# Handing an activation tile over in quarters, two PSUM banks exchanged, and a final norm by token sums in a two-block float32 transformer kernel

## What the kernel computes

```python
# first block, per layer
h = rmsnorm(x, g_mix);  z = h @ w_in                 # 12 column groups
y_a = latent attention (lora norms, w_q_up, w_kv_up, rotary, causal softmax)
y_b = sc_b * causal_dwconv(sc_c * sc_h, w_sc)        # 3 taps
u   = causal_dwconv(cf_a * sigmoid(cf_g), w_cf, b_cf)  # 31 taps, 512 channels
y_c = silu(layernorm(u));  y_d = retention
x = x + concat(y_a, y_b, y_c, y_d) @ w_o
uf = causal_dwconv(rmsnorm(x, g_ffn) @ w_up, w_ffn_conv)
x = x + (silu(gate) * up) @ w_down
x = x + (p @ w_pe) * sigmoid(rmsnorm(x, g_pe) @ w_pg)
# second block, per layer: rmsnorm, w_in_2, four attention-like mixers, gates
x = x + mixed @ w_out_2
# at the end
out = rms_norm(x, final_norm_g_2)                    # mean over the channels of a token
```

## Time and profile before

| | us |
|---|---|
| median of 3 runs (range) | 3526.3 (3523.01 to 3529.35) |
| profiled execution | 3530.64 |
| its span, first to last instruction | 3528.8 |

### The profile page before, as it was taken

How to read it: one execution, slowest core, us unless ns; L and a number is a source line. 1 busy time by engine, 2 the same in 40 slices (tenths; PEclk the granted TensorE clock), 3 DMA queues, 4 the chain that set the end, 5 groups by cost and what they waited for, 6 DMA issues and landing times. The chain is left out here.

```text
span 3528.8 us, 55547 instructions
## 1 busy us (share of the span) xinstructions
PE 3441.4 (98%) x21156; PEld 3019.1 (86%) x21156; DVE 2642.3 (75%) x3441; ACT 1467.2 (42%) x1488; POOL 982.2 (28%) x763
## 2 busy tenths in 40 slices
PE   8999999999999999999999999999999999999998
PEld 7899888888888888998888888888888888888887
DVE  7876688787776768766887777867667766677775
ACT  5434444343433543344443434335444444444442
POOL 0751433121123426714322121214231004040004
PEclk9899999999999999999999999999999999999999
DMA  6344455555555544344555555555443445443453
GB/s 225 132 142 163 173 191 191 174 196 177 202 175 189 178 163 149 133 166 171 186 190 171 199 177 203 173 188 187 169 164 134 155 168 183 168 150 128 156 179 141
DMA packets 90063, 605.10 MB, mean 171 GB/s; under 512 B 10000, under 2 KB 10160, under 8 KB 28592
## 3 DMA queue, kind: packets, MB, share of 16 engines
q1 hardware_dynamic: 88992, 599.83, 48.7%
q10 hardware_dynamic: 912, 3.11, 0.2%
HBM read 600.80 MB, written 2.10 MB: 171 GB/s over the span
## 5 line engine op out<-in xcount | busy, mean ns | idle before, releaser
L549 PE MATMUL bank<-H,whi 128*128 128x512 f32 x6784 | 2419.6, 401 | 51.5 <-DVE H L1462 37.6
L553 PE MATMUL bank<-H,wlo 128*128 128x256 f32 x7552 | 2126.5, 282 | 0.0
L549 PEld LDWEIGHTS bank<-H,whi 128*128 128x128 f32 x6784 | 1282.8, 189 | 371.3 <-DVE wlo L1412 38.1
L1041 ACT ACTIVATE whi<-raw 128x2048 fp32r<-128x2048 f32 (+1 forms) x610 | 1095.5, 1796 | 1199.5 <-DMA raw<-in_slabs_down 268.2
L1412 DVE TENSOR_TENSOR wlo<-raw,whi 128x2048 fp32r<-128x2048 f32 (+1 forms) x610 | 1337.6, 2193 | 185.2 <-ACT whi L1041 181.4
L553 PEld LDWEIGHTS bank<-H,wlo 128*128 128x128 f32 x7552 | 1437.9, 190 | 0.5
L549 PE MATMUL bank<-G,whi 128*128 128x512 f32 x1408 | 495.4, 395 | 0.0
L466 POOL TENSOR_TENSOR sqtmp<-tmp 128x256 f32<-128x256 f32 x88 | 219.1, 2490 | 888.4 <-DVE tmp L1980 888.4
L553 PE MATMUL bank<-G,wlo 128*128 128x256 f32 x1408 | 396.1, 281 | 0.0
L549 PEld LDWEIGHTS bank<-G,whi 128*128 128x128 f32 x1408 | 264.7, 188 | 62.9
L553 PEld LDWEIGHTS bank<-G,wlo 128*128 128x128 f32 x1408 | 264.1, 188 | 0.0
(11 more groups left out here) (318 smaller groups left out, 2481.6 us busy)
## 6 DMA issues: line engine op xcount, KB each, us to landing
raw<-in_slabs_up SPq DMA_DIRECT2D x176, 1024.0 KB, 4.8
raw<-in_slabs_down SPq DMA_DIRECT2D x128, 704.0 KB, 4.0
raw<-in_slabs_wo SPq DMA_DIRECT2D x32, 1024.0 KB, 4.8
raw<-in_slabs_pg SPq DMA_DIRECT2D x32, 1024.0 KB, 4.8
raw<-in_slabs_gates SPq DMA_DIRECT2D x32, 1024.0 KB, 4.8
raw<-in_slabs_wout SPq DMA_DIRECT2D x32, 1024.0 KB, 4.8
raw<-in_slabs_sc SPq DMA_DIRECT2D x24, 1024.0 KB, 4.8
raw<-in_slabs_fox SPq DMA_DIRECT2D x24, 1024.0 KB, 4.8
```

The costliest lines, as they stand in the source:

```text
L549: pe.matmul(b[0:r.m, :], whi[:, n % RAW, w], r.src[:, k, :], start=at == 0, stop=False)
L553: last = pe.matmul(b[0:r.m, 0:T], wlo[:, n % RAW, w], r.src[:, k, 0:T], start=False, stop=at == r.kt - 1)
L1041: act.activation(whi[:, n % RAW, 0:w], raw[:, n % RAW, 0:w], ACT.Copy).then_inc(S("hi_ready"), 1)
```

## The change

Four edits. (1) The runs wo, last down, pg and wout get an unrolled tail of four slabs on every engine (`tail`). At the last slab of each, ACT writes high chunks 0 to 11 as PE frees H a quarter at a time (`h_free`, raised behind chunks 3, 7 and 11 of the last slab; no such wait after down, whose product doesn't read H), and chunks 12 to 15 behind the last slab; the rounding of the slab three ahead comes after both. DVE writes low chunks 0 to 11 before it waits for the last slab, evicts that slab, writes 12 to 15, and splits the slab ahead after that. (2) In pe, unit 0 goes to the slab banks, with a wait for the eviction of the slab that used each, unit 1 to the auxiliary ones. (3) The output norm: ACT scales the chunks by the gain during the last slab, squares chunk 15 itself; PE sums over partitions and chunks with tokens on partitions (two products with one column for POOL's 15 chunks, two for chunk 15), root and reciprocal are of 128x2 values, two products spread them, and DVE multiplies four times 128x1024. (4) Taps: 5 (was 4) in cfa, 3 (was 8) behind kv, qn, qr, 2 at each ret slab but the first (was 4 at the last two only).

```diff
     # Run.__init__
-        self.head = 0
+        self.head = self.tail = 0
+    HANDED = ("wo", "pg", "wout", "rg", "gates")
+        if key[0] in HANDED[:3] or key[0] == "down" and key[2] == NG - 1:
+            by[key].tail = 4
+        if key[0] in HANDED:
+            h_free[key] = 3 * len(h_free)
     # groups
-        full = (r.count - tail) // 4 if r.loop else 0
+        full = (r.count - max(tail, r.tail)) // 4 if r.loop else 0
     # SP, output; POOL, last sum
-            sp.wait_ge(S("final_chunk"), 4 * k + 4)
+            sp.wait_ge(S("final_four"), k + 1)
-            square_sum(slab_of(("wout", l)))
+            square_sum(slab_of(("wout", l)), DC if l == 0 else DC - 1)
     # PE, run
-                    if key[0] in ("gates", "rg") and 4 * i + j == r.count - 1 and at in (3, 7, 11):
+                    if key[0] in HANDED and isinstance(i, int) and 4 * i + j == r.count - 1 and at in (3, 7, 11):
                         last.then_inc(S("h_free"), 1)
     # PE, both_units
-                if u:
-                    pe.wait_ge(S("evac"), r.first)
                 for p in range(4):
-                    b = bank[(r.first + 2 + p) % 4] if u else aux[p]
+                    if u == 0:
+                        pe.wait_ge(S("evac"), r.first - 1 + min(p, 1))
+                    b = aux[p] if u else bank[(r.first + 2 + p) % 4]
     # PE, gate_norm, and pg's wait for its bank
-            pe.wait_ge(S("pe_taken"), 6 * l + 3)
-            pe.wait_ge(S("evac"), by["pe", l].first + 1)
+            pe.wait_ge(S("evac"), by["pe", l].first + 2)
-            ... free=lambda j, l=l: pe.wait_ge(S("pe_taken"), 6 * l + 4 + min(j, 2)))
+            ... free=lambda j, l=l: pe.wait_ge(S("pe_taken"), 6 * l + 1 + min(j, 2)))
     # PE, end
-        norm_sum()
+        pe.wait_ge(S("square_sum"), nth("norm") - 1)
+        for t in range(2):
+            pe.matmul((pS, pT)[t][:, 0:1], sqacc[:, t * P:(t + 1) * P], ones[:, 0:1], start=True, stop=False, ...)
+        pe.wait_ge(S("last_square"), 1)
+        for t in range(2):
+            last = pe.matmul((pS, pT)[t][:, 0:1], w4[:, 0, t * P:(t + 1) * P], ones[:, 0:1], start=False, stop=True, ...)
+        last.then_inc(S("last_sums"), 1)
+        pe.wait_ge(S("last_inverse"), 1)
+        for t in range(2):
+            last = pe.matmul(pX[:, t * P:(t + 1) * P], inv_rms[:, t:t + 1].to_broadcast([P, P]), C("ident"), ...)
+        last.then_inc(S("last_spread"), 1)
     # ACT, run
+                handing = last is not None and isinstance(i, int) and 4 * i + j == r.count - 1
+                if handing:
+                    last(0, 12)
+                    yield i, j
+                    last(12, DC)
                 split_hi(r, i, j, AHEAD)
+                if handing:
+                    continue
     # ACT, x_hi
+        def x_hi(g, l, name, base, lo=0, hi=DC, handed=None):
+            for c in range(lo, hi):
+                if handed is not None:
+                    r = by[handed]
+                    act.wait_ge(*((S("h_free"), h_free[handed] + c // 4 + 1) if c < (10 if handed[0] == "wout" else 12)
+                                  else (S("slab_done"), r.first + r.count)))
     # ACT, during the last slab
+        def scaled_outputs(lo, hi):
+            for c in range(lo, hi):
+                act.wait_ge(S("evac"), by["wout", L - 1].first + c + 1)
+                if c == DC - 1:
+                    act.activation(w4[:, 0, :], x[:, c, :], ACT.Square).then_inc(S("last_square"), 1)
+                act.activation(z[:, c, :], x[:, c, :], ACT.Copy,
+                               scale=col("final_norm_g_2", 0, c)).then_inc(S("scaled_x"), 1)
     # DVE, run
+                handing = last is not None and isinstance(i, int) and 4 * i + j == r.count - 1
+                if handing:
+                    last(0, 12)
                 dve.wait_ge(S("slab_done"), r.first + j + 4 * i + 1)
                 yield i, j, bank[(r.first + j) % 4]
+                if handing:
+                    last(12, DC)
     # DVE, taps: to_z (ret), cfa, and kv, qn, qr
-                advance(taps, 4 if 4 * i + j in (6, 7) else 0)
+                advance(taps, 0 if 4 * i + j == 0 else 2)
-                    advance(taps, 4)
+                    advance(taps, 5)
-                    advance(taps, 8)
+                    advance(taps, 3)
     # DVE, end
-        inverse()
-        for c in range(DC):
-            dve.scalar_tensor_tensor(z[:, c, :], x[:, c, :], col("final_norm_g_2", 0, c), rms[:], ...)
+        dve.wait_ge(S("last_root"), 1)
+        dve.reciprocal(inv_rms[:, 0:2], inv_rms[:, 0:2]).then_inc(S("last_inverse"), 1)
+        dve.wait_ge(S("last_spread"), 1)
+        dve.wait_ge(S("scaled_x"), DC)
+        token = pX[:, 0:T].rearrange("p (a t) -> p a t", a=1).to_broadcast([P, 4, T])
+        for k in range(4):
+            four = z[:, 4 * k:4 * k + 4, :]
+            dve.tensor_tensor(four, four, token, ALU.mult).then_inc(S("final_four"), 1)
```

More of the change, by code:

```diff
@@ L323, in col @@
         return cols[:, at:at + 1]
-    runs, by = [], {}
+    HANDED = ("wo", "pg", "wout", "rg", "gates")
+    runs, by, h_free = [], {}, {}
     sources = {"qn": cq, "qr": cq, "kv": cq[:, 4:6, :]}
@@ L425, in _, with square_sum @@
         done = {"sq": 0, "add": 0, "norm": 0, "g": 0, "tap": 0}
-        def square_sum(final):
+        def square_sum(final, chunks=DC):
             done["norm"] += 1
@@ L434, in square_sum @@
                 pool.wait_ge(S("cf_pool"), done["tap"])
-            for c in range(DC):
+            for c in range(chunks):
                 pool.wait_ge(*final(c))
@@ L444, in square_sum @@
                     ins = pool.tensor_tensor(sqacc[:], sqacc[:], sqtmp[:], ALU.add)
-                    if c < DC - 1:
+                    if c < chunks - 1:
                         ins.then_inc(S("pool_add"), 1)
@@ L1041, in split_hi, with run @@
             act.activation(whi[:, n % RAW, 0:w], raw[:, n % RAW, 0:w], ACT.Copy).then_inc(S("hi_ready"), 1)
-        def run(key, beside=None, base=None):
+        def run(key, beside=None, base=None, last=None):
             r = by[key]
@@ L1335, in _ @@
                     pass
-            for _ in run(("wo", l)):
+            for _ in run(("wo", l), last=lambda lo, hi, l=l: x_hi("g_ffn", l, "evac", by["wo", l].first, lo, hi, ("wo", l))):
                 pass
-            x_hi("g_ffn", l, "evac", by["wo", l].first)
             for g in range(NG + 1):
@@ L1353, in _, with handing @@
                 if g:
-                    for _ in run(("down", l, g - 1)):
+                    def handing(lo, hi, l=l):
+                        x_hi("g_pe", l, "evac", by["down", l, NG - 1].first, lo, hi)
+                    for _ in run(("down", l, g - 1), last=handing if g == NG else None):
                         pass
-            x_hi("g_pe", l, "evac", by["down", l, NG - 1].first)
             for _, u in run(("pe", l)):
@@ L1359, in _ @@
                     act.wait_ge(S("pe_out"), 6 * l + 3 * u + p + 1)
-                    b = bank[(by["pe", l].first + 2 + p) % 4] if u else aux[p]
+                    b = aux[p] if u else bank[(by["pe", l].first + 2 + p) % 4]
                     act.activation(z[:, 8 * u + 2 * p:8 * u + 2 * p + 2, :].rearrange("p a t -> p (a t)"), b[:],
                                    ACT.Copy).then_inc(S("pe_taken"), 1)
-            for i, j in run(("pg", l)):
+            for i, j in run(("pg", l), last=lambda lo, hi, l=l: x_hi(*following(l), "gated", DC * l, lo, hi, ("pg", l))):
                 if isinstance(i, int) and i == 0 and j == 0:
@@ L1381, in _, with handing @@
                 y_split(l, k)
-            for _ in run(("wout", l)):
+            handing = scaled_outputs
+            if l == 0:
+                def handing(lo, hi):
+                    x_hi("norm_g_2", 1, "evac", by["wout", 0].first, lo, hi, ("wout", 0))
+            for _ in run(("wout", l), last=handing):
                 pass
             if l == 0:
-                x_hi("norm_g_2", 1, "evac", by["wout", l].first)
-            norm()
+                norm()
+        act.wait_ge(S("last_sums"), 1)
+        for t in range(2):
+            last = act.activation(inv_rms[:, t:t + 1], (pS, pT)[t][:, 0:1], ACT.Sqrt, scale=1.0 / D, bias=eps[:])
+        last.then_inc(S("last_root"), 1)
     @block.vector
@@ L1455, in invert, with x_lo @@
             dve.reciprocal(inv_rms[:, 0:columns], inv_rms[:, 0:columns]).then_inc(S("inverted"), 1)
-        def x_lo(g, l):
-            h0 = DC * (nth("h") - 1)
-            for c in range(DC):
+        def x_lo(g, l, lo=0, hi=DC):
+            h0 = DC * ((cnt["h"] if lo else nth("h")) - 1)
+            for c in range(lo, hi):
                 dve.wait_ge(S("h_hi"), h0 + c + 1)
@@ L1474, in y_lo, with residual @@
                                   ALU.subtract).then_inc(S("h_ready"), 1)
-        def residual(key):
-            for i, j, b in run(key):
+        def residual(key, last=None):
+            for i, j, b in run(key, last=last):
```

(17 more changed lines are left out.)

21 lines of the change are left out of this document (12 added, 9 removed).

## The result

The changed kernel takes 3503.6 us, median of 5 runs (3500.9 to 3509.8), beside 3525.3 for the kernel before in the same session: a ratio of 0.9942, 95% interval 0.9929 to 0.9955. That is 21.8 us less by the medians (by the interval 16 to 25), and 23.6 by the two profiled spans (3528.8 and 3505.2). The forecast was 28.0 less. One of the four executions of the run "square behind the chunks" took 9235.8 us at a granted clock of 0.52; the figures of that run leave it out.

The account below looks back on a forecast made before the run. PE bounds the kernel, busy 3441.4 of 3528.8 us; other engines matter only where it waits. Terms 16.2 + 7.0 - 4.3 + 5 + 4.1 = 28.0 us off 3526.3 gave 3498, range 3484 to 3511.

Parts of the forecast that it names:

- wout to gla: Handover from wout to gla's first slab: low chunks written before the last slab's eviction save 4.9 us.
- pg to zq and gla: Handovers behind pg: 3.5 us saved each, 7.0 together, with a 2.7 us wait at chunk 12 and a clock fall.
- Wo to up: Handover from wo to up's first slab: PE restarts without a pause, saving 5.7 us in layer 0, 5.6 in layer 1.
- The slack of 0.2: Up's fourth slab: its low half ready about 423.6, slab starting 423.8; a slow split would eat this margin.
- Down to pg: Unit 0 waits for the last down slab's late eviction: loses 1.8 us in layer 0, 2.5 in layer 1.
- banks as aimed: Rival: eviction before DVE's low chunks, so unit 0 doesn't wait; 17 us more saved, 3481 us; chance 0.07.
- Taps: Cfa to head scores: redistributed taps save 5.0 us less 1 in layer 1, 1.7 in layer 0, less 0.7; sum 5.
- Norm: Output norm at the kernel's end: time behind PE's end falls from 16.8 to 12.7 us, saving 4.1.
- Clock stays up: Rival: no clock fall in the short new pauses, so 38 us saved, 3488 us; chance 0.19.
- Long queue: Rival: DVE's low chunks before the eviction delay splits and taps, so 15 us saved, 3511 us; chance 0.15.
- Starved PE: Rival: fetching the unrolled tails' instructions starves PE; at 4.5 us per run the time is 3534 us; chance 0.02.

Follow-up runs that it names:

- square behind the chunks: Against the kernel with the down tile written whole, POOL squares chunk 15 only after DVE's last low chunk: 3489.8 us, ratio 0.9889.
- the run with the tile whole: Changed kernel, but the last down slab's tile is written whole behind the run, as before the change: 3491.4 us, ratio 0.9901.
- the fastest kernel: Changed kernel with down tile whole, fewer taps ahead of kv, p's low halves behind kv, layer 0 taps 2 behind kv, qn, qr and 5 per score slab: 3475.6 us.

## Why the prediction came out as it did

The mechanisms held and the time fell in the range, 5.6 us above the forecast. The gain was forecast too large: 28.0 lies above the 16 to 25 that the measurement allows. It was not saved by errors that cancel: every term came out below its forecast, by 0.1 (wout to gla) to 2.4 (pg to zq and gla). Step by step:

- **Wo to up, 5.7 and 5.6: mis-sized.** Measured 4.9 and 4.8 in the first slab. The term was "four more chunks 1.6"; they take 2.51, since POOL squares and adds chunk 15 at the same time (0.79 and 0.80). Left out, they take 1.67 and the slab is 0.84 shorter. The forecast had counted DVE alone. The slack of 0.2 at up's fourth slab held: PE has no listed wait there.
- **Wout to gla, 4.9: right.** First slab 12.06 to 7.22, 4.8; the stage shows 4.1 because its eight slabs ran at the slower pace.
- **Pg to zq and gla, 3.5 each: mis-sized, 2.2 and 2.4.** The first slab gained 2.95 and 3.3, the second lost 0.8 and 0.95 (6.75 and 7.03 instead of 5.98 and 6.08). The same four chunks are 0.9 late; the pause is 2.21 where 2.7 was forecast, and the clock did fall behind it, into the second slab: over the 6.5 us from 1263.50 the granted clock is 0.74.

```profile
1263.50:1270.00 6.50, 6.07 (x23) 0.74 0.34 105
```

- **Down to pg, a loss of 1.8 and 2.5: right.** Pauses of 6.22 and 6.3 where 6.7 was said, none before pg, a loss of 1.4 (at equal pace) and 2.95 in the two profiles. Against the mean of the four layers with old banks and whole tiles (106.6 at equal pace) it is 2.4 a layer, where 2.15 was forecast. The forecast named DVE's order as what decides, and the run with the tile whole shows it: the rival "banks as aimed" priced this at 17 us, and it brings 13.5 in the profile, 12 by medians.
- **Taps, 5: near in size, not in its split.** Forecast 1.7 and 4 by layer, less 0.7; found 2.1 and 1.8, together 3.9. The pauses came as said: kv 5.90 and 2.25 (5.4 and 2.1 forecast), scores 1.07 and 1.17 (1.3 each), none at the spread. What layer 1 gained there it gave back in part at kv: kv to qr grew from 18.8 to 21.7, and only 5.0 came back in ret.
- **Norm, 4.1: nearly right, 3.7** in the profiled pair, 3.3 on the mean of two executions with the old norm (107.9, 107.4) and nine with the new (104.1 to 104.7). The products take 1.15 each (1.2 forecast); the rest of the difference is hops and stores, 3.5 us behind the last product where 3.0 had been put.
- **Rivals.** Clock stays up: out for this kernel, it fell behind both 2.2 us pauses of its profile, though not behind every such pause (last section). Banks as aimed: its condition, an early eviction, was not met, as the forecast had said. Long queue: out. Starved PE: out; the eight unrolled tails show no pause.

Sum of what was measured with the pace taken out: 4.9 + 4.8 + 4.8 + 2.2 + 2.4 - 4.8 + 3.9 + 3.3 = 21.5, beside the 21.8 of the medians. Of the 6.5 that the forecast had more, 4.1 are in the five handovers to up, zq and gla, where the overlap with POOL costs 0.5 to 0.8 each and is most of it, 1.1 in the taps, 0.8 in the norm and 0.5 at down to pg. No run takes back only the quarters at wo, pg and wout, or only the norm: these terms rest on the lengths of stages and on the pauses in them.

## What to carry to other kernels

Two edits that each gain can lose together when both move the same instruction: before a tile is handed over in quarters, look what else waits for the eviction that goes behind them, and whether the next consumer needs the tile at once (p's units did not). Price an operation by a row in which the other engines do what they will do beside it. And compare stages, over several executions and at the same pace of the loops, before a change of a few microseconds is called measured.

## What the hardware showed that was not expected

**Matmuls of one loop run at one of two paces at full clock.** Windows of 100 us inside up, all with PE busy throughout and a granted clock of 1.00; the count of matmuls differs by 2%. Kernel before, in up's second and third group of layer 0:

```profile
535.00:635.00 100.00, 100.00 (x579) 1.00 0.54 189
725.00:825.00 100.00, 100.00 (x567) 1.00 0.54 189
```

and the kernel after in the same windows, in which it runs the same groups:

```profile
535.00:635.00 100.00, 100.00 (x567) 1.00 0.54 183
725.00:825.00 100.00, 100.00 (x579) 1.00 0.55 189
```

A run of 22 slabs takes 122.03 or 124.37 us, a slab of 16 pairs 5.55 or 5.65, in every kernel of this study. The pace stays through a run and changes between runs; which run gets which differs between executions of the same code (up's second group of layer 0 took 124.37 in the changed kernel and 122.03 in the one with old taps, whose instructions there are the same). What sets it is open. Eight groups of up at 2.34 us and eight of down at 0.77 can move an execution by several microseconds, as much as one of the terms here. Pg is a case of its own: its slabs took 5.65 us in two of the four layers of the two kernels in which pg is one loop, and 5.55 in all 20 layers of the ten kernels in which its last four slabs are unrolled. Whether the unrolling does it, no run tests.

**Low stretches without a pause.** Low stretches of 3.4 or 6.8 us follow the 2.2 us pause before the thirteenth chunk of zq and of gla in 14 of 20 places (ten kernels, two layers), as the rows of before had suggested; in the other six the granted clock stays at 1.00. None follows the pauses of 1.4 and 1.7 us in p's first unit with the tile whole. But in the fastest kernel the records of the granted clock hold two low stretches between kv and ret of layer 0 and one in layer 1, though PE has no pause above 0.8 us there. The first, with the stretch ahead of it:

```profile
118.90:122.30 3.40, 3.40 (x29) 1.00 0.43 104
122.30:125.70 3.40, 3.40 (x18) 0.50 0.49 207
```

PE is busy in both, and does 18 matmuls at 1.2 GHz where it had done 29 at 2.4. What PE did before them, other than work in the smaller tiles of these stages, no row shows.
